# Side-by-side gate weights, finer waits in the first two pieces, and an earlier last row product in a two-layer decoder trunk

## What is computed

```python
def rmsnorm(x, g):
    y = x * lax.rsqrt(jnp.mean(x * x, axis=-1, keepdims=True) + NORM_EPS)
    return y * g

# layer 1: 36 gate logits per token come out of the input projection of 2048
q, kc, vc, ks, vs, kw, vw, g_logit, q_mem = split_cols(h @ w_in, ...)
gates = jax.nn.sigmoid(g_logit).reshape(B, S, 12, 3)

# layer 0, first product of the kernel
km, vm = split_cols(rmsnorm(mem, norm_g[i, 4]) @ w_kv, [512, 512])

# every layer
x = x + rmsnorm(attn, norm_g[i, 1])
f = conv_ffn(rmsnorm(x, norm_g[i, 2]), w_gate, w_up, conv_w, conv_b, w_down)
x = x + rmsnorm(f, norm_g[i, 3])
```

## Time and profile before

| | us |
|---|---|
| median of 3 runs | 2240.47 (2240.29 to 2240.64) |
| the profiled execution's own time | 2240.5 |
| its span, first to last instruction | 2238.6 |
| TensorE busy in it | 2227.5 |
| VectorE busy | 1594.8 |
| ScalarE busy | 1151.7 |

### The profile page before, as it was taken

How to read it: one execution, slowest core, us unless ns; L and a number is a source line. 1 busy time by engine, 2 the same in 40 slices (tenths; PEclk the granted TensorE clock), 3 DMA queues, 4 the chain that set the end, 5 groups by cost and what they waited for, 6 DMA issues and landing times.

```text
span 2238.6 us, 26396 instructions
## 1 busy us (share of the span) xinstructions
PE 2227.5 (100%) x10172; PEld 1838.7 (82%) x10172; DVE 1594.8 (71%) x2163; ACT 1151.7 (51%) x1558; POOL 18.7 (1%) x20
## 2 busy tenths in 40 slices
PE   9999999999999999999999999999999999999998
PEld 7888888888888888888888887788888888888887
DVE  7777675788888888544566678757888888784444
ACT  7556674654454544444574554456544454544443
POOL 0000000000000000000030000000000000000000
PEclk9999999999999999999999999999999999999999
DMA  9554555677776777676655843356776777766664
GB/s 329 182 172 155 180 174 191 206 229 224 237 233 224 233 227 236 196 228 196 194 179 178 270 141 104 123 179 189 245 237 224 234 222 238 237 215 205 191 196 150
DMA packets 128285, 459.00 MB, mean 205 GB/s; under 512 B 14784, under 2 KB 17088, under 8 KB 127392
## 3 DMA queue, kind: packets, MB, share of 16 engines
q1 hardware_dynamic: 127888, 456.78, 63.3%
q0 software_dynamic: 128, 0.48, 0.1%
q10 hardware_dynamic: 144, 0.05, 0.0%
HBM read 443.71 MB, written 2.10 MB: 199 GB/s over the span
## 4 chain that ended last, share of the span: by engine, by line
PE 98%; DVE 1%; ACT 0%; DMA 0%; issue 0%; SPq 0%; DVEq 0%; ACTq 0%
PE bank L580 97%; PE bank L703 0%; DVE lo L1194 0%; PE bank L717 0%; DMA raw<-in_mem 0%; DVE x L1324 0%; PE bank L750 0%; PE bank L842 0%; PE bank L849 0%; ACT h L964 0%; DVE x L1357 0%; ACT mf L1038 0%; DVE y L1320 0%; DVE h L1232 0%; ACT root L1040 0%
## 5 line engine op out<-in xcount | busy, mean ns | idle before, releaser
L1194 DVE TENSOR_TENSOR lo<-raw,hi 128x1024 fp32r<-128x1024 f32 x776 | 945.1, 1223 | 511.1 <-ACT hi L921 504.9
L580 PE MATMUL bank<-hi,h 128*128 128x512 f32 x3904 | 1226.9, 392 | 0.4 <-ACT h L964 0.4
L921 ACT ACTIVATE hi<-raw 128x1024 fp32r<-128x1024 f32 x776 | 817.1, 1058 | 785.9 <-PE bank L580 756.6
L580 PEld LDWEIGHTS bank<-hi,h 128*128 128x128 f32 x3904 | 732.9, 188 | 151.7 <-issue 0.9
L580 PE MATMUL bank<-lo,h 128*128 128x512 f32 x1952 | 760.1, 389 | 0.0
L580 PE MATMUL bank<-hi,mid 128*128 128x512 f32 x1408 | 434.0, 389 | 0.0
L580 PEld LDWEIGHTS bank<-lo,h 128*128 128x128 f32 x1952 | 366.7, 188 | 74.1
L580 PEld LDWEIGHTS bank<-hi,mid 128*128 128x128 f32 x1408 | 264.3, 188 | 55.1
L580 PE MATMUL bank<-lo,mid 128*128 128x512 f32 x704 | 273.9, 389 | 0.0
L580 PE MATMUL bank<-hi,o 128*128 128x512 f32 x512 | 163.8, 394 | 0.0
L1437 DVE STREAM_TRANSPOSE cv<-mf 32x256 f32<-32x256 f32 x352 | 154.0, 437 | 6.4
(11 more groups left out here) (231 smaller groups left out, 1213.5 us busy)
## 6 DMA issues: line engine op xcount, KB each, us to landing
raw<-in_gate SPq DMA_DIRECT2D x176, 512.0 KB, 4.2
raw<-in_up SPq DMA_DIRECT2D x176, 512.0 KB, 3.6
raw<-in_down SPq DMA_DIRECT2D x176, 512.0 KB, 4.2
raw<-in_in SPq DMA_DIRECT2D x136, 512.0 KB, 4.1
raw<-in_out SPq DMA_DIRECT2D x64, 512.0 KB, 3.9
taps<-in_taps SPq DMA_DIRECT2D x44, 512.0 KB, 5.4
raw<-in_mem SPq DMA_DIRECT2D x31, 512.0 KB, 4.2
st<-st SPq DMA_DIRECT2D x22, 448.0 KB
```

Source lines behind the costliest of these rows:

```text
L580: return mm(out, lhsT, rhs, start=first, stop=last, skip_group_check=True)
L921: act(hi[k][:, 0:w], raw[k][:, 0:w], ACT.Copy).then_inc(hi_done, 1)
L1194: tt(lo[k][:, 0:w], raw[k][:, 0:w], hi[k][:, 0:w].bitcast(F32), ALU.subtract).then_inc(lo_done, 1)
```

## The change

- **Gates.** ACT writes the rounded gate weights to `gw[:, :, 0:36]` and DVE the remainders to `gw[:, :, 36:72]`, so that one matmul of 72 stationary columns gives both products with `h_hi`, and one of 36 that with `h_lo`: 32 matmuls for 48. The bank holds [72, 256], and the two halves are added when it is turned: the two transposes become two f32 matmuls against `gsum`, two unit matrices on each other, loaded by a third DMA on POOL's queue.
- **First piece.** `first_memory` takes the products of a half for both token tiles term by term, and waits ahead of each term for what that term reads.
- **Second piece.** Rounded and split in two halves; PE waits for the first half's remainder (`second_wlo`) and, between the halves, for the second's.
- **End.** `last_gain` of the last norm moves from behind the first add to the place between the sum and the reciprocal, for both token tiles.

```diff
+        gw, = region([("gw", [P, DT, 96], F32R)])
-        sb("line", [P, 88])
+        gsum = sb("gsum", [P, 3 * HEADS])
+        sb("line", [P, 52])
-        SMALL = 16 * 2
+        SMALL = 16 * 3
...
-                if n == 0:
-                    pe_.wait_ge(first_wlo, 1)
-                    pe_.wait_ge(first_mlo, 1)
-                elif c.gate and c.gate[0] == "m":
+                if c.gate and c.gate[0] == "m":
...
-                    if (n, q) == (0, 1):
-                        pe_.wait_ge(lo_done, 1)
-                        pe_.wait_ge(mlo_done, 1)
+                    if (n, q) == (1, 1):
+                        pe_.wait_ge(lo_done, 2)
...
+            def first_memory(c):
+
+                take_banks(c)
+                for q in range(2):
+                    w_hi, w_lo = (w[0][:, q * W:(q + 1) * W] for w in (hi, lo))
+                    pe_.wait_ge(*((hi_done, 1) if q else (first_whi, 1)))
+                    pe_.wait_ge(*((mhi_done, 1) if q else (first_mhi, 1)))
+                    for t in range(2):
+                        add(B[c.banks[t]][:, :], amem[:, q, 0, half(t)], w_hi, q == 0, False)
+                    pe_.wait_ge(*((lo_done, 1) if q else (first_wlo, 1)))
+                    for t in range(2):
+                        add(B[c.banks[t]][:, :], amem[:, q, 0, half(t)], w_lo, False, False)
+                    pe_.wait_ge(*((mlo_done, 1) if q else (first_mlo, 1)))
+                    for t in range(2):
+                        m = add(B[c.banks[t]][:, :], amem[:, q, 1, half(t)], w_hi, False, False)
+                m.then_inc(piece_done, 1)
...
-                out = B[b][0:3 * HEADS, 0:T]
                 for kt in range(DT):
-                    at = slice(kt * 3 * HEADS, (kt + 1) * 3 * HEADS)
-                    add(out, hi[k][:, at], h[:, kt, 0, :], kt == 0, False)
-                    add(out, hi[k][:, at], h[:, kt, 1, :], False, False)
-                    m = add(out, lo[k][:, at], h[:, kt, 0, :], False, kt == DT - 1)
+                    add(B[b][0:6 * HEADS, 0:T], gw[:, kt, 0:6 * HEADS], h[:, kt, 0, :], kt == 0, False)
+                    m = add(B[b][0:3 * HEADS, 0:T], gw[:, kt, 0:3 * HEADS], h[:, kt, 1, :], False, kt == DT - 1)
...
-                    m = tr(B[5][:, t * 3 * HEADS:(t + 1) * 3 * HEADS], gt[0:3 * HEADS, half(t)],
-                           ident[0:3 * HEADS, 0:3 * HEADS])
+                    m = add(B[5][:, t * 3 * HEADS:(t + 1) * 3 * HEADS], gt[0:6 * HEADS, half(t)],
+                            gsum[0:6 * HEADS, :], t == 0)
...
+                if n == 1:
+                    act(hi[1][:, 0:W], raw[1][:, 0:W], ACT.Copy).then_inc(second_whi, 1)
+                    act(hi[1][:, W:2 * W], raw[1][:, W:2 * W], ACT.Copy).then_inc(hi_done, 1)
+                    return
+                if c.kind == "gates":
+                    act(gw[:, :, 0:3 * HEADS], raw[k][:, 0:w].rearrange("p (a g) -> p a g", a=DT), ACT.Copy).then_inc(hi_done, 1)
+                    return
...
+                if n == 1:
+                    dve.wait_ge(second_whi, 1)
+                    tt(lo[1][:, 0:W], raw[1][:, 0:W], hi[1][:, 0:W].bitcast(F32), ALU.subtract).then_inc(second_wlo, 1)
+                    dve.wait_ge(hi_done, 2)
+                    tt(lo[1][:, W:2 * W], raw[1][:, W:2 * W], hi[1][:, W:2 * W].bitcast(F32), ALU.subtract)\
+                        .then_inc(lo_done, 1)
+                    return
...
+                if k == 3:
+                    last_gain(k, t)
                 dve.wait_ge(root_y, n)
...
                     m = first_add(3, t, j)
                 m.then_inc(x_new, 1)
-                last_gain(3, t)
...
             pool.dma_start(msk[:], A["masks"]).then_inc(s_small, 16)
+            pool.dma_start(gsum[0:6 * HEADS, :], A["gate_sum"]).then_inc(s_small, 16)
```

More of the change, by code:

```diff
@@ L438, in build @@
         first_whi, first_wlo, first_mhi, first_mlo = (sem(n) for n in ("first_whi", "first_wlo", "first_mhi", "first_mlo"))
+        second_whi, second_wlo = sem("second_whi"), sem("second_wlo")
         s_row, s_l1, s_out = sem("s_row"), sem("s_l1"), sem("s_out")
@@ L662, in gates @@
             def gates(c, p, n):
-                b, k = c.banks[0], n % RING
+                b = c.banks[0]
                 take(b, gt_done, 1)
-                out = B[b][0:3 * HEADS, 0:T]
                 for kt in range(DT):
-                    at = slice(kt * 3 * HEADS, (kt + 1) * 3 * HEADS)
-                    add(out, hi[k][:, at], h[:, kt, 0, :], kt == 0, False)
-                    add(out, hi[k][:, at], h[:, kt, 1, :], False, False)
-                    m = add(out, lo[k][:, at], h[:, kt, 0, :], False, kt == DT - 1)
+                    add(B[b][0:6 * HEADS, 0:T], gw[:, kt, 0:6 * HEADS], h[:, kt, 0, :], kt == 0, False)
+                    m = add(B[b][0:3 * HEADS, 0:T], gw[:, kt, 0:3 * HEADS], h[:, kt, 1, :], False, kt == DT - 1)
                 m.then_inc(piece_done, 1)
@@ L875, in _ @@
             for n, (c, p) in enumerate(PLAN.pieces):
-                if n:
+                if n == 1:
+                    pe_.wait_ge(second_wlo, 1)
+                elif n:
                     pe_.wait_ge(lo_done, n + 1)
-                if n in APART:
+                if n == 0:
+                    first_memory(c)
+                elif n in APART:
                     apart(c, p, n)
@@ L1108, in gates @@
                 act_.wait_ge(piece_done, PLAN.at("gates") + 1)
-                act(gt[0:3 * HEADS, :], B[4][0:3 * HEADS, 0:T], ACT.Copy).then_inc(gt_done, 1)
+                act(gt[0:6 * HEADS, :], B[4][0:6 * HEADS, 0:T], ACT.Copy).then_inc(gt_done, 1)
             def gatesT():
@@ L1192, in split_piece @@
                 k, w = n % RING, size(c)
+                if n == 1:
+                    dve.wait_ge(second_whi, 1)
[4 more added lines that the diff above has]
+                    return
                 dve.wait_ge(hi_done, n + 1)
+                if c.kind == "gates":
+                    tt(gw[:, :, 3 * HEADS:6 * HEADS], raw[k][:, 0:w].rearrange("p (a g) -> p a g", a=DT),
+                       gw[:, :, 0:3 * HEADS].bitcast(F32), ALU.subtract).then_inc(lo_done, 1)
+                    return
                 tt(lo[k][:, 0:w], raw[k][:, 0:w], hi[k][:, 0:w].bitcast(F32), ALU.subtract).then_inc(lo_done, 1)
@@ L1632 @@
     arrays["taps"] = np.broadcast_to(taps.reshape(2, 4, PAIRS, W).transpose(0, 2, 1, 3)[:, :, None], (2, PAIRS, P, 4, W))
+    arrays["gate_sum"] = np.concatenate([np.eye(3 * HEADS), np.eye(3 * HEADS)]).astype(np.float32)
     arrays["zeros"] = np.zeros((1, 2, W), np.float32)
```

## The result

The changed kernel takes 2259.05 us (2258.94 to 2259.93), against 2240.47 us (2240.29 to 2240.64) before: a ratio of 1.0084, 95% interval 1.0069 to 1.0099. The forecast was 2238.6, so the measured time lies 20.5 us above it. The profiled execution has a span of 2257.1 us against 2238.6, at a granted clock of 0.999.

A forecast was written before the change was run, and what follows sets the result against it. TensorE was taken as the bound, busy 2227.5 us of a 2238.6 us span. The terms -1.85 + 0.32 + 0.0 - 0.33 = -1.86 took 2240.5 to 2238.6 us, range 2237.5 to 2239.6.

The forecast's parts named there:

- Everything in between moves forward as a block, if nothing else is late next: TensorE's work between the start and the last matmul: savings there pass on in full; no size of its own.
- All rivals: Four other outcomes: start pays too (2237.6 us, 10%), gates don't shrink (3%), clock falls back (3%), something late or tail colliding (12%).
- Gates: Gate matmuls: 32 steps in 3.71 us instead of 48 in 5.56, so -1.85 us (bounds -1.75 and -1.86).
- Transposition of the gates: Two f32 matmuls replacing the gates' two transposes: gap 0.75 us instead of 0.43, so +0.32 us (bounds 0 and +0.45).
- the twin: Two similar f32 matmuls already in the kernel, 60 rows against 30 columns, whose gap of 0.75 us was taken as model.
- The estimate of 0.1 us: Gates' transposition: extra cost by the skill's rule alone, 6 x 36 columns more; it would have given 2238.4 us in total.
- Start: First two pieces: they end about 1.0 us earlier, but piece 2 waits for DVE's memory remainder; 0.0 us (bounds -1.0, +0.1).
- the first half of piece 0 can't gain: Start of the kernel: taking operands as they come doesn't help this half, whose last matmul ends at 7.86 us.
- End: After the last matmul: moving the last row product ahead of the reciprocal saves 0.33 us (bounds -0.4 and 0).
- the gates shrank: Gate matmuls: the opposing rival had steps growing with stationary columns, 5.57 us as before, result 2240.5 us; chance 3%.
- no step of 0.42 came back after 9 us: Start: the opposing rival had TensorE's clock halving again in a new rest before piece 2, result 2241.5 us; chance 3%.
- nothing behind the gates was late: Behind the gates: the opposing rival had something late there, or the tail's outputs colliding, 2238.9 to 2239.5 us; chance 12%.

The follow-up runs named there:

- e1: The changed kernel with the unused spacer `line` cut from 52 to 48 floats, putting the tensors behind it back at their old addresses: 2238.37 us, ratio 0.999.
- e10: As e1, but with the first two pieces as in the kernel before: 2238.46 us, ratio 0.9991.
- e7: Probe without the kernel's computation: groups of 36 matmuls, stationary side, moving side or both moved in 32-byte steps up to 512; 389 to 396 ns a matmul.
- e4: Probe without the kernel's computation: groups of 36 back-to-back matmuls at various operand offsets, repeated with DVE copying beside the first ones; 389 to 395 ns at 32-byte shifts.
- e12: Probe without the kernel's computation: operand offsets alternating between matmuls, then other widths, bf16 and small offsets; 389 to 397 ns in the alternating groups, 379 in bf16.
- e5: The kernel before with every tensor, activations and weights alike, moved by 32 bytes: 2240.86 us, ratio 1.0.

## Why the prediction was wrong

**The step that failed** is the sentence "Everything in between moves forward as a block, if nothing else is late next". It took for granted that a matmul which the diff doesn't touch costs what it cost, and none of its bounds had a term for that step. All rivals were about waits, counts and the clock. The two lines of the diff on `line` and `gsum` were priced at nothing, without a word: they looked like bookkeeping, and they hold the whole result. The size that was missing is 20.7 us, 6.3 ns on each of 3264 matmuls (e1 against the changed kernel). No row shown of before could tell it. Its wide groups do differ in their mean, 389 ns with `mid` against 394 with `o` and 397 with `amem`, but these differences have another cause: in e1, where all distances are multiples of 256 bytes, they are still 389, 394 and 396. Only the same group before and after the shift shows the effect. The Trainium skill (SBUF — State Buffer, Operand start alignment) states only that an operand must start at a multiple of its element size, and says of that rule "This is about legality, not speed"; all offsets tried here are legal by it. What an offset costs it doesn't say; the runs do.

**Gates: right.** In the changed kernel itself the first gate matmul and the next wide one are here:

```profile
1201.61 1.58 PE L583 MATMUL bank<-h,gw 128*72 128x256 f32 x12
...
1205.39 0.40 PE L583 MATMUL bank<-hi,h 128*128 128x512 f32 x1
```

The two starts are 3.78 us apart for 32 steps, 0.118 each, between the bounds of 3.71 and 3.81, where the earlier trace rows had 5.56: -1.78 for -1.85. Rounding and remainder in strides took 0.69 and 0.76 us, three pieces ahead, and nobody waited.

**Transposition of the gates: the size was off.** The forecast took the gap of the twin, 0.75 us, for the 0.43 of before. The rows of e1 are

```profile
1198.90 0.39 PE L583 MATMUL bank<-hi,h 128*128 128x512 f32 x1
1199.13 0.53 PE L583 MATMUL bank<-gsum,gt 72*128 72x36 f32 x4
...
1199.81 0.39 PE L583 MATMUL bank<-lo,h 128*128 128x512 f32 x1
```

By the forecast's own way of reading, the gap runs from 1198.90 + 0.227 = 1199.13 to 1199.81 - 0.227 = 1199.58: 0.45 us. So +0.02 for +0.32: nearly the lower bound, "if the extra passes hide in the gap that the transposes make already". Four records for two f32 products were forecast rightly, but the gap that they make is nearly that of the transposes. The estimate of 0.1 us, by what the Trainium skill (TensorE: Matmul & The Clock Gate, Terms) says of transpose mode, was nearer than the twin, but still too high. Why the twin's gap is larger no run shows.

**Start: right in what it was worth, with some luck on the way.** Piece 0's last two matmuls, piece 1's first, the memory remainder, and piece 2's first:

```profile
8.75 0.63 PE L583 MATMUL bank<-hi,amem 128*128 128x512 f32 x2
...
9.78 0.50 PE L583 MATMUL bank<-hi,amem 128*128 128x512 f32 x1 [0.41 <-DVE lo L1219]
...
12.51 0.88 DVE L1237 SCALAR_TENSOR_TENSOR amem<-memT,gains,amem 128x256 fp32r<-128x256 f32 x2
...
13.54 0.47 PE L583 MATMUL bank<-hi,amem 128*128 128x512 f32 x1 [0.69 <-DVE amem L1237]
```

Piece 0 ends at 8.75 + 2 x 0.23 = 9.21 (9.22 was forecast), piece 1 starts at 9.78 (9.79), and what it gained turns into the wait for DVE's `amem`: piece 2 begins at 13.54, its second matmul at 13.84, where before had 13.78; in e1 that is 13.78 too. The agreement at 9.22 is chance. The prediction held that the first half of piece 0 can't gain; its last matmul starts at 7.25 in the changed kernel, and at 7.63 before, since the steps of 0.42 end sooner. But this is no gain of the edit: in e10, with the old start, they end sooner too (last matmul of that half at 6.99). The second half then waits for ACT's `amem`, and e1 ends piece 0 at 8.90. Piece 2's operands take up such differences, though not always all of them: in e10 piece 1 runs until piece 2 starts, and the second matmul of piece 2 comes at 14.08. So the finer waits were worth nothing against the profiled execution of before, and 0.3 us against that of e10. The slower steps of piece 1 don't show either: the wait takes them up (0.69 us here, 0.77 in e1).

**End: right.** The last wide matmul of before, and then e1 from its own on:

```profile
2230.94 0.39 PE L580 MATMUL bank<-hi,mid 128*128 128x512 f32 x1
```

```profile
2229.28 0.39 PE L583 MATMUL bank<-hi,mid 128*128 128x512 f32 x1
...
2230.56 0.68 DVE L1357 TENSOR_TENSOR y<-bank,row_h 128x512 f32<-128x512 f32 x1
2230.68 0.29 ACT L1064 ACTIVATE root<-tot,cst 128x1 f32<-128x1 f32 x1 [0.23 <-DVE tot L1348]
2231.16 0.15 DVE L1352 RECIPROCAL rpost<-root 128x1 f32<-128x1 f32 x1
```

The reciprocal starts 0.48 us behind the root's start, against 0.33 in the earlier trace rows, and the end comes 2236.6 - 2229.28 = 7.32 us behind the last wide matmul, where before had 2238.6 - 2230.94 = 7.66: -0.34 for -0.33.

**The sum** of these rows is -1.78 + 0.02 + 0.0 - 0.34 = -2.1 us. e1 has 2.4 against the kernel before on the same chip, and 2.0 in the spans of the two profiled executions, which were on different chips. So with the addresses restored the forecast of 2238.6 is met within 0.2 us, although the transposition had been priced 0.3 too high. The rivals all stayed away: the gates shrank, no step of 0.42 came back after 9 us, and nothing behind the gates was late.

## What to carry to other kernels

Where wide matmuls of 4-byte rounded operands fill TensorE, keep the stationary and the moving tensors at multiples of 32 bytes, and at starts that are equal modulo 256 bytes. After any edit of the allocations, also of a tensor that nobody reads, compute the new addresses of what lies behind it, with the rounding of each; and treat a spacer of odd length as a tuned number. In the profile the sign of it is a group of matmuls whose mean has grown by some ns over the same group in the kernel before, without more idle time ahead: compare the groups by form and operands, one by one, and not the waits, which show nothing here. Different groups of one kernel aren't to be compared for this, since they differ for other causes too (389 with `mid` and 394 with `o` in e1).

## What the runs showed of the hardware

- A back-to-back matmul of 128 stationary and 512 moving columns of 4-byte rounded data takes 389 to 390 ns on the page when its two operands' starts are multiples of 32 bytes and differ by a multiple of 256, and 391 to 396 at other distances that are multiples of 32, in a constant stream. The mean step with `mid` is 226.7 ns in the kernel before and 233.3 in the changed one; in the map (e7) it is 226.7 to 227.8 and 228.8 to 234.3.
- Below 32 bytes equal offsets don't help in general: with both sides moved by 4 bytes the page reads 399 to 400 ns, by 8, 12, 16, 20 and 24 bytes 393, 390, 392 to 393, 397 and 396. 4 bytes on the moving side alone read 399.
- The mean of the records isn't always the step. 4 bytes on the stationary side read 394 ns in e4 and 399 in e12, but the starts lie 232.5 and 232.3 ns apart. Where it matters, measure from start to start.
- The loads of the stationary side have the same duration in either case: 188 ns in the group with `hi` and `mid` before and after, and 187 to 189 in the groups of the map. What grows is the matmul's own step.
- The step also has a type in it. 36 bf16 matmuls of this shape take 180.81 - 173.03 = 7.78 us from the start of one group to the next, 216 ns each, and rounded 4-byte ones at the best offset 226.7. The Trainium skill (TensorE: Matmul & The Clock Gate, Back-to-back issue gap) gives N / 2.4 + 2.5 ns as the gap of an isolated matmul, 216 ns for 512 columns, and about 131 ns for a sustained stream. The bf16 row agrees with the first; the 4-byte rows, 226.7 and 233.3 ns, lie above it, and no row here is near the second.
- What clashes inside is **open**. It needs no second engine (e4), it depends on the distance of the two sides in a constant stream (e5, e7), and in an alternating one neither the matmul's own pair nor the next load against the present stream accounts for the times (e12). That the next stationary side has a part in it, as the 30 places behind e12 suggest, is not shown by a run of its own.
